# Two-block transformer kernel: the modulation vectors multiplied on VectorE, lanes added on TensorE

## The reference

```python
silu_c = jax.nn.silu(c)
silu_cc = jax.nn.silu(c_ctx)
for l in range(DEPTH_2):
    mod = silu_c @ w_mod[l] + b_mod[l]
    shift, scale, gate = jnp.split(mod[:, None, :], 3, axis=-1)
    cmod = silu_cc @ w_mod[l] + b_mod[l]
    cshift, cscale, cgate = jnp.split(cmod, 3)
    h = rmsnorm(x, norm_g[l]) * (1.0 + scale) + shift
    hc = rmsnorm(cx, norm_g[l]) * (1.0 + cscale) + cshift
    ...
    x = x + gate * (y @ w_o[l])
```

## Time and profile before

| what | value |
| --- | --- |
| runs, median (lowest to highest) | 3526.9 us (3526.59 to 3531.01) |
| the profiled execution: its time, its span | 3526.57 us, 3524.8 us |
| mean granted TensorE clock | 0.967 of full |
| busy share of the span: PE, DVE, ACT, POOL | 93%, 50%, 42%, 6% |
| chain that ended last: PE, DVE, ACT, DMA | 84%, 6%, 3%, 2% |
| matmuls with `MV` | 768, 640 of them in the MLP |
| chunks split | 986 |
| moved by DMA | 628 MB, mean 178 GB/s |

### The profile page before, as it was taken

How to read it: one execution, slowest core, us unless ns; L and a number is a source line. 1 busy time by engine, 2 the same in 40 slices (tenths; PEclk the granted TensorE clock), 3 DMA queues, 4 the chain that set the end, 5 groups by cost and what they waited for, 6 DMA issues and landing times.

```text
span 3524.8 us, 39356 instructions
## 1 busy us (share of the span) xinstructions
PE 3270.7 (93%) x15208; PEld 2636.2 (75%) x15208; DVE 1746.3 (50%) x2482; ACT 1472.7 (42%) x2183; POOL 224.1 (6%) x332
## 2 busy tenths in 40 slices
...
GB/s 186 284 206 220 266 144 162 150 215 219 205 267 245 251 223 264 266 243 251 229 193 126 127 72 97 109 100 129 100 127 122 99 78 184 178 140 127 211 186 125
DMA packets 353237, 628.10 MB, mean 178 GB/s; under 512 B 42571, under 2 KB 109816, under 8 KB 350236
## 3 DMA queue, kind: packets, MB, share of 16 engines
...
...
## 4 chain that ended last, share of the span: by engine, by line
PE 84%; DVE 6%; ACT 3%; issue 2%; DMA 2%; POOL 1%; ACTq 1%; SPq 0%; DVEq 0%; POOLq 0%
PE acc L414 25%; PE acc L419 22%; PE acc L418 22%; PE acc L1095 4%; PE acc L1122 3%; DVE w_lo L395 3%; PE acc L416 2%; PE acc L1110 2%; ACT w_hi L389 1%; PE acc L1079 1%; PE acc L743 1%; PE acc L1099 1%; ACTq L1255 1%; PE acc L651 1%; ACT stage L468 0%
## 5 line engine op out<-in xcount | busy, mean ns | idle before, releaser
L414 PE MATMUL acc<-w_hi,a_hi 128*128 128x512 f32 (+4 forms) x3800 | 1511.6, 398 | 40.4 <-issue 20.8
L395 DVE TENSOR_TENSOR w_lo<-raw,w_hi 128x1024 fp32r<-128x1024 f32 (+2 forms) x986 | 1161.0, 1208 | 749.0 <-ACT w_hi L389 731.7
L419 PE MATMUL acc<-w_hi,a_lo 128*128 128x512 f32 (+4 forms) x3800 | 1474.1, 388 | 0.0
L418 PE MATMUL acc<-w_lo,a_hi 128*128 128x512 f32 (+4 forms) x3800 | 1473.8, 388 | 0.0
L389 ACT ACTIVATE w_hi<-raw 128x1024 fp32r<-128x1024 f32 (+2 forms) x986 | 1000.5, 1044 | 744.9 <-PE acc L419 723.0
L414 PEld LDWEIGHTS acc<-w_hi,a_hi 128*128 128x128 f32 x3800 | 720.3, 190 | 206.4 <-DVE w_lo L395 38.0
L419 PEld LDWEIGHTS acc<-w_hi,a_lo 128*128 128x128 f32 x3800 | 719.1, 189 | 147.5
L418 PEld LDWEIGHTS acc<-w_lo,a_hi 128*128 128x128 f32 x3800 | 720.3, 190 | 131.5 <-issue 0.7
L1219 DVE TENSOR_REDUCE at_st<-acc 128x1 f32<-128x256 f32 (+3 forms) x208 | 101.2, 487 | 452.6 <-PE acc L1095 307.1
L1152 ACT ACTIVATE pb<-acc,at_st 128x256 f32<-128x256 f32 (+3 forms) x208 | 108.3, 521 | 382.8 <-DVE at_st L1219 359.1
L414 PE MATMUL acc<-w_hi,MV 128*128 128x512 f32 x384 | 155.9, 406 | 5.4 <-DVE w_lo L395 2.6
...
...
## 6 DMA issues: line engine op xcount, KB each, us to landing
...
raw<-in_w_mlp_in SPq DMA_DIRECT2D x128, 512.0 KB, 4.5
raw<-in_w_mlp_out SPq DMA_DIRECT2D x128, 512.0 KB, 5.3
raw<-in_e_w_in SPq DMA_DIRECT2D x104, 512.0 KB, 5.3
...
```

The source lines that it names most:

```text
L395: nc.vector.tensor_tensor(w_lo[:, n % SPLITS, 0:size], raw[:, n % RAWS, 0:size], w_hi[:, n % SPLITS, 0:size].bitcast(F32), ALU.subtract)\
L414: nc.tensor.matmul(o, s.lhs(0, kt, tt), wh, start=kt == 0, stop=False)
L418: nc.tensor.matmul(o, s.lhs(0, kt, tt), wl, start=False, stop=False)
L419: last = nc.tensor.matmul(o, s.lhs(1, kt, tt), wh, start=False, stop=end)
```

## The change

20 of the 24 modulation groups leave TensorE. The matrix is now cut into 10 **pieces** of 1024 columns, each 16 chunks of one k tile (128 x 1024, 512 KB, the same bytes). For each chunk VectorE does two SCALAR_TENSOR_TENSOR: the raw chunk times `ct[:, k, v]` (one number for each lane), added to the running sum `lanes[:, v, :]`, for both vectors v. No split is needed. After 16 chunks the 128 lanes still have to be added: TensorE takes `lanes`, 128 columns at a time, as the stationary side against a column of ones (16 matmuls 128x1 in plain f32, `lanes_add`), and ScalarE copies the result to `mc` (`lanes_keep`), already in the layout that the feeds read. POOL loads a bias row for each piece into lane 0 (`vec_bias`).

The places are fixed by a table: two pieces in qkv (from step 1), qkv_end and gates_a, one chunk every 2.5 chunks of the stage; two in branch (from step 3) and out1, six in mlp steps 1 to 27, one chunk every second chunk, and of every 36 places 32 and 34 stay empty. A piece's lane sum stands behind place 40 (qkv) or 32 of its stretch. `MODF` keeps only the gates; `vec_pool` and the second `mod_pool` go. Nine of ScalarE's small loads at the start go to POOL, after the identity is built.

```diff
+        self.width, self.wtiles, self.mods = width, wtiles, {}
 
     def order(self):
 
-        return [(g, c) for c in range(len(self.chunks)) for g in self.groups()]
+        out = []
+        for c in range(len(self.chunks)):
+            out += [(self, c)] + self.mods.get(c, [])
+        return out
...
+class Matvec:
+    def __init__(self, pieces):
+        self.pieces = pieces
+        self.raw = {}
+    def chunk(self, q):
+        W, n0 = self.pieces[q // KT]
+        return W.rearrange("(k p) n -> p k n", p=P)[:, q % KT, n0:n0 + CH]
...
-                for s_, m in zip(ins[1:], mod_steps(0, 3, 3 * it)):
-                    s_.beside(m)
-                for s_, m in zip(outs[2:], mod_steps(1, 2, 2 * it)):
-                    s_.beside(m)
...
+        vecs = Matvec([(A["w_mod_2"][0], j * CH) for j in range(6)] + [(A["w_mod_2"][1], j * CH) for j in range(4)])
+        NQ = len(vecs.pieces)
+        spots = [("qkv", i, c) for i in range(1, 10) for c in range(8)] + [("qkv_end", 0, c) for c in range(8)] + \
+                [("gates_a", i, c) for i in range(2) for c in range(8)]
+        late = [("branch", i, c) for i in range(3, 12) for c in range(4)] + \
+               [("out1", i, c) for i in range(4) for c in range(8)] + [("mlp", i, c) for i in range(28) for c in range(8)]
+        vec_spots = [spots[46 * j + 5 * i // 2] for j in range(2) for i in range(KT)] + \
+                    [late[36 * j + 2 * i] for j in range(2) for i in range(KT)] + \
+                    [late[76 + 36 * j + 2 * i] for j in range(6) for i in range(KT)]
+        lane_spots = [spots[46 * j + 40] for j in range(2)] + [late[36 * j + 32] for j in range(2)] + \
+                     [late[76 + 36 * j + 32] for j in range(6)]
+        for q, (name, i, c) in enumerate(vec_spots):
+            stages[name].steps[i].mods.setdefault(c, []).append((vecs, q))
+        raw_users = count_stages([stages[n] for n in order])
...
-            n = g.no[c]
+            n = g.raw[c]
             if n >= RAWS:
-                sp.wait_ge(lo_ready, n - RAWS + 1)
-            dst = raw[:, n % RAWS, 0:g.wtiles * g.width].rearrange("p (k n) -> p k n", k=g.wtiles)
-            sp.dma_start(dst, g.chunks[c]).then_inc(landed[n % RAWS], 16)
+                split, m = raw_users[n - RAWS]
+                if split:
+                    sp.wait_ge(lo_ready, m + 1)
+                else:
+                    sp.wait_ge(vec_ctx, m + 1)
+                    sp.wait_ge(vec_x, m + 1)
+            if g is vecs:
+                sp.dma_start(raw[:, n % RAWS, :], vecs.chunk(c)).then_inc(landed[n % RAWS], 16)
+            else:
+                dst = raw[:, n % RAWS, 0:g.wtiles * g.width].rearrange("p (k n) -> p k n", k=g.wtiles)
+                sp.dma_start(dst, g.chunks[c]).then_inc(landed[n % RAWS], 16)
...
+        def vec_add(dve, q):
+
+            j, k = q // KT, q % KT
+            vec_landed(dve, q)
+            if k == 0:
+                vec_begin(dve, j)
+            for v, done in ((0, vec_ctx), (1, vec_x)):
+                if k:
+                    dve.wait_ge(done, q)
+                t = lanes[j >= 2][:, v, :]
+                nc.vector.scalar_tensor_tensor(out=t, in0=raw[:, vecs.raw[q] % RAWS, :], scalar=ct[:, k, v:v + 1],
+                                               in1=bias_row[j >= 2][:, :] if k == 0 else t, op0=ALU.mult,
+                                               op1=ALU.add).then_inc(done, 1)
+
+        def vec_bias(pool, j):
+
+            if j not in (0, 2):
+                pool.wait_ge(vec_ctx, KT * (j - 1) + 1)
+                pool.wait_ge(vec_x, KT * (j - 1) + 1)
+            else:
+                nc.gpsimd.memset(bias_row[j >= 2][:, :], 0.0).then_inc(bias_zero, 1)
+                pool.wait_ge(bias_zero, j // 2 + 1)
+            layer, c = (0, j * CH) if j < 6 else (1, (j - 6) * CH)
+            pool.dma_start(bias_row[j >= 2][0:1, :], A["b_mod_2"][layer:layer + 1, c:c + CH]).then_inc(bias_in, 16)
+
...
+        def lanes_add(pe, j):
+
+            pe.wait_ge(vec_ctx, KT * (j + 1))
+            pe.wait_ge(vec_x, KT * (j + 1))
+            if j:
+                pe.wait_ge(lanes_out, j)
+            for v in range(2):
+                for n in range(CH // P):
+                    last = nc.tensor.matmul(acc[:, 4, 8 * v + n:8 * v + n + 1], lanes[j >= 2][:, v, n * P:(n + 1) * P],
+                                            ones[:, 0:1], start=True, stop=True)
+            last.then_inc(lanes_done, 1)
+
+        def lanes_keep(act, j):
+            act.wait_ge(lanes_done, j + 1)
+            layer, c = (0, 8 * j) if j < 6 else (1, 8 * (j - 6))
+            nc.scalar.activation(mc[:, layer, :, c:c + 8], acc[:, 4, 0:16].rearrange("p (v n) -> p v n", v=2), ACT.Copy)\
+              .then_inc(lanes_out, 1)
+
+        for j, (name, i, c) in enumerate(lane_spots):
+            stages[name].hook("pe", i, c, lambda pe, j=j: lanes_add(pe, j))
+            stages[name].hook("act", i, c + 1 if c + 1 < len(stages[name].steps[i].chunks) else c,
+                              lambda act, j=j: lanes_keep(act, j))
...
                 if s is not None:
                     for g, c in s.order():
-                        if g is not s or c:
-                            split(eng, g, c)
-                        if g is s:
-                            st.run_hooks(which, i, c, eng)
-                        if c == 5 and g is s and i and steps[i - 1].evac["kind"] == "relu2":
+                        if g is vecs:
+                            if which == "dve":
+                                vec_add(eng, c)
+                            continue
+                        if c:
+                            split(eng, s, c)
+                        st.run_hooks(which, i, c, eng)
+                        if c == 5 and i and steps[i - 1].evac["kind"] == "relu2":
...
+            for dst, src in ((onehot_t[:, :], C["onehot"]), (relb_t[:, :], A["rel_bias"]), (bmask_t[:, :], C["bmask"])):
+                act.dma_start(dst, src).then_inc(setup_in, 16)
+
+        def setup_pool_loads(pool):
...
+            setup_pool_loads(pool)
+            vec_bias(pool, 0)
...
             pool_stream(pool, stages["in2"])
+            next_norm(pool)
             at2.pool(pool)
-            mod_pool(pool, 1, 1, [(4, stages["mlp"].upto["put", 4])], 0, 2 * DM)
-            vec_pool(pool, 1)
             g6_pool(pool)
```

More of the change, by code:

```diff
@@ L77, in run_hooks @@
             f(eng)
+class Matvec:
[5 more added lines that the diff above has]
+        return W.rearrange("(k p) n -> p k n", p=P)[:, q % KT, n0:n0 + CH]
 def count_stages(stages):
-    total = {"relu2": 1}
+    total, raw = {"relu2": 1}, []
     for st in stages:
         for s in st.steps:
-            for g in s.groups():
-                g.no, g.fill, g.put, g.done = {}, {}, {}, {}
+            s.no, s.raw, s.fill, s.put, s.done = {}, {}, {}, {}, {}
@@ L87, in count_stages @@
             for g, c in s.order():
-                g.no[c] = total.get("chunk", 0)
-                total["chunk"] = g.no[c] + 1
-            for g in s.groups():
-                for bank, _ in g.tiles[:-1]:
-                    g.done[bank] = total.get(("done", bank), 0)
-                    total[("done", bank)] = g.done[bank] + 1
-                for bank, _ in g.tiles:
-                    g.fill[bank] = total.get(("fill", bank), 0)
-                    total[("fill", bank)] = g.fill[bank] + 1
-                    if g.evac["kind"] == "store":
-                        g.put[bank] = total.get(("put", bank), 0)
-                        total[("put", bank)] = g.put[bank] + 1
-                for kind in ("relu2", "branch"):
-                    if g.evac["kind"] == kind:
-                        g.nth = total.get(kind, 0)
-                        total[kind] = g.nth + 1
+                g.raw[c] = len(raw)
@@ new lines, in count_stages @@
+                if g is s:
+                    s.no[c] = total.get("chunk", 0)
+                    total["chunk"] = s.no[c] + 1
+                raw.append((g is s, s.no[c] if g is s else c))
+            for bank, _ in s.tiles[:-1]:
+                s.done[bank] = total.get(("done", bank), 0)
+                total[("done", bank)] = s.done[bank] + 1
+            for bank, _ in s.tiles:
+                s.fill[bank] = total.get(("fill", bank), 0)
+                total[("fill", bank)] = s.fill[bank] + 1
+                if s.evac["kind"] == "store":
+                    s.put[bank] = total.get(("put", bank), 0)
+                    total[("put", bank)] = s.put[bank] + 1
@@ L104, in count_stages @@
+            for kind in ("relu2", "branch"):
+                if s.evac["kind"] == kind:
+                    s.nth = total.get(kind, 0)
+                    total[kind] = s.nth + 1
         st.upto = dict(total)
-    return total
+    return raw
 class Unit:
@@ L427, in pe_stream @@
             for i, s in enumerate(st.steps):
[L428 to L429 removed]
+                for c in range(len(s.chunks)):
```

(12 more changed lines are left out.)

190 lines of the change are left out of this document (102 added, 88 removed).

## The result

The changed kernel takes **3483.2 us** (median of 4 runs, 3475.4 to 3488.4), the kernel before 3526.7 beside it: ratio 0.987, 95% interval 0.985 to 0.990. It is faster, clear of the noise but by less than 2%: 43.5 us, or 1.2%, where 83 us were forecast. The profiled execution took 3488.4, its span is 3486.5, 38.3 less than before.

A forecast was written before the change was run, and what follows sets the result against it. The prediction took TensorE, busy for 93% of the span, to bound the kernel. Gains of 185.9 us less costs of 102.8 gave a net 83.1 off 3526.6, so 3443 us, with a range of 3408 to 3488.

The forecast's parts named there:

- rival 1: Behind each lane sum the clock falls, as one-column matmuls count as idling: 17.5 us in all, time 3461, chance 0.3.
- signs of being wrong: Pairs above 2.5 us, lane sums above 5.5, clock 0.5 behind them, raw-chunk waits over 12 us, waits in plain MLP steps.
- start: At the kernel's start, nine loads leave ScalarE for POOL, so TensorE starts near 10.8 us: 20.3 us gained.
- modulation leaves the MLP: In the MLP, 160 chunks of 4 modulation matmuls leave TensorE's queue: 159.5 us gained over four passes.
- POOL before out2: After block two's attention, POOL starts its gate product earlier without the modulation work: 6.1 us gained.
- additions from branch on: In branch, out1 and MLP, pairs of additions delay `w_lo` behind evacuations or feeds: costs 16.1, 22.4 and 13.8 us.
- additions at chunk 1 in qkv: In the qkv stages, only an addition at chunk 1 delays the next `w_lo`, by about 0.9: costs 3.6 us.
- DMA: In the qkv stages, same bytes, 32 more chunks while `BROW` is written, mostly covered by the ring: 4 us, bounds 0 and 12.
- lane sums: TensorE adds the lanes ten times, 16 plain f32 matmuls each, 3.9 us a sum: costs 39 us, bounds 30 and 57.
- lanes with `hidden`: In mlp steps 9, 18 and 27, where `hidden` follows `lanes_keep`, ScalarE's lost lead costs 3.9 us.
- rival 4: At the start, POOL's issues or raw chunks hold it to 27 us, so no gain there: time 3463, chance 0.08.
- rivals 2 and 3: VectorE's additions: 2, mostly covered by ring and splits, 3414, chance 0.15; 3, VectorE becomes the bound, about 3616, chance 0.02.

The follow-up runs named there:

- e1: The changed kernel with each matmul of a lane sum reading 128 columns of ones instead of 1: 3469.6 us, ratio 0.985.
- e3: The changed kernel with one matmul of 16 columns in place of a lane sum's 16 matmuls, output not the reference's: 3439.1 us, ratio 0.975.
- e6: The changed kernel with the 128 additions from the branch on moved, none behind an evacuation at chunk 0 or a feed before chunk 3: 3420.5 us, ratio 0.970.
- e4: The changed kernel with 150 of the 160 pairs of additions cut from 1024 to 64 columns, chunks still loaded: 3429.4 us, ratio 0.972.
- e8: The changed kernel with POOL's nine small start loads waiting until raw buffers 4 to 7 have landed: 3475.1 us, ratio 0.986.

## Why the prediction was right and wrong

Forecast 3443, measured 3483.2: the sign and the mechanism were right, the gain was overrated almost twofold, and the result lies near the upper end of the range, which rival 1 had widened; the slowest of its four runs, 3488.4, is at that end. 18 us of the shortfall (`first_gate` and qkv0) come from effects that neither the sum nor the range had, so that it stayed inside is in part luck. Two of the prediction's own signs of being wrong appeared: a clock of 0.50 behind the sums, and a wait of ScalarE for a raw chunk of over 12 us (13.8). Against the terms of the sum, measured by steps on the two traces and on e1 and e3:

| term | forecast | measured |
|---|---|---|
| start | -20.3 | -14.3 (19.8 at the first matmul, 5.5 lost in qkv0) |
| modulation leaves the MLP | -159.5 | -160.7 |
| POOL before out2 | -6.1 | -8.2 |
| additions from branch on | 52.3 | 60.0 |
| additions at chunk 1 in qkv | 3.6 | 1.8 |
| DMA | 4 | 9.4 (qkv step 3) |
| lane sums | 39 | 33.5, and 15.1 of clock |
| lanes with `hidden` | 3.9 | 4.5 |
| `first_gate` | 0 | 12.7 |
| sum | -83.1 | -46.2 |

The modulation's gain is 891.1 less 16 x (23.13 + 21.76) and 12.1 for what only the last step holds; the additions' cost is that of the steps without a sum in e3 against before: 24.7 in the branch, 18.4 in out1 and 9 x 1.88 in the MLP. The two spans differ by 38.3, so 7.9 are in no term. Of these, 4.6 lie in branch steps 3 to 10 and out1, compared with e3: branch step 5 and out1 steps 0 and 2 are each 1.4 to 1.6 us longer in the changed kernel's trace (so is branch step 3, but e3 loses the same in step 4). That is the clock again. Two stretches of branch step 3, in the changed kernel:

```profile
746.00:750.00 4.00, 1.99 (x9) 1.36 (x8) 4.00 (x4) 1.06 (x1) 0.72 (x2) 0.99 0.54 177
749.90:753.30 3.40, 3.40 (x10) 2.63 (x9) 3.40 (x4) 0.00 (x0) 0.00 (x0) 0.50 0.94 285
```

TensorE, waiting for the additions, was busy for only 1.99 of 4 us, and the granted clock was 0.50 behind it; the other three steps have such a stretch too. Before, none of them has, nor has branch or out1 step 0, 1 or 3 in e6, where the additions stand elsewhere. So an addition at a boundary now and then costs the clock besides its length. Of the rest, 2.5 are behind out2, within the scatter of that part.

**Start, modulation, POOL, `hidden`.** The first matmul comes as forecast, so rival 4 is out, and the other three are right within 2.1 us.

**Additions.** Right in place and mechanism: rivals 2 and 3 are out. What the sum lacked is the clock behind some of these waits, the 4.6 us above and part of the 60.0. A pair is 2.47 instead of 2.3, within its bounds; a boundary costs 1.88 for 1.6 (MLP), 2.42 for 2.3 (branch), 4.1 for 3.9 (out1). e4 and e6 show the same from two sides: take the additions' length away and 54 us go, move them off these places and 63 go (some 53 by the places) with all the work still done.

**Lane sums.** The term had two errors of opposite sign. 3.9 a sum was too much (3.35 by e1 against e3). "An MLP pass with its groups of 8 short transposes stays at 1.00" was the argument by which I gave the fall of the clock only 0.3, and it fails: those were 8 transposes of 128 columns among other matmuls, the sum is 32 matmuls in a row of one column. Rival 1 forecast 17.5 us for it; 15.1 were measured, with a clock of 0.50 for 3.4 or 6.8 us behind eight of the ten sums. The Trainium skill ("TensorE: Matmul & The Clock Gate", What's actually happening) says that activity releases the clock. In the traces here TensorE was busy for all 3.90 us of a sum of one column each and the clock was 0.50 behind it, and for all 3.30 us of one of 128 columns with 1.00 behind it.

**DMA.** "The bytes are the same" was the step that failed. I costed transfers by bytes alone. In qkv step 3 that went wrong only in size: full DMA at 348 GB/s, 9.4 us for 4, within the bounds of 0 and 12, and not all of it DMA's, as the clock was 0.89 there. `first_gate` I hadn't costed at all: two stores of 8 KB cost 12.7 us, because behind them raw chunks land after 14 us and the ring of eight raw buffers does not last so long; 10.1 of it are TensorE's wait, the rest goes at the low clock behind it. Why such small transfers hold up large ones stays open: their number of packets alone doesn't do it, and POOL's queue as the cause is untested. The start is the same omission: I asked how long POOL's issues take (7.5 us, hidden, as forecast), and not what they do to the transfers they stand beside; that is 5.5 us, and e8 gets it back. With "the bytes" I had also left out the queue: nine loads had moved from ScalarE's to POOL's.
